# Two mixer and feed-forward layers written out, their modulation sums placed anew, and ScalarE's gates, Silus and root tables regrouped

## The chip, the cores and the metric

The kernel runs on one core of a Trainium2 chip. TensorE multiplies into PSUM banks; VectorE, ScalarE and GpSimd each work through a list of their own, in order; SyncE issues all DMAs here. The engines meet at semaphores. The metric is the device time of one execution in microseconds, lower is better.

## The reference

The program is a stack of two parts. Only the first, `first_block`, is touched by the change. All data is fp32, 256 tokens of width 1024. Cut to what matters:

```python
c_act = silu(c)
for l in range(2):                                     # DEPTH
    mod = c_act @ ada_w[l] + ada_b[l]                  # 6 x 1024: sh1 sc1 g1 sh2 sc2 g2
    h = rmsnorm(x, norm_mix_w[l]) * (1 + sc1) + sh1
    x = x + g1 * mixer(h)
    h = rmsnorm(x, norm_ffn_w[l]) * (1 + sc2) + sh2
    u = causal_dwconv(h @ w_up[l], conv_w, conv_b)     # width 2 x 2816, 3 taps
    a, val = split(u, 2)
    x = x + g2 * ((gelu(a) * val) @ w_down[l])

def mixer(h):
    # proj = h @ w_in: latents of attention, q/k/v of the mLSTM, o, its gates, g_mla, g_mlstm
    y_mla   = attention(rmsnorm(c_q) @ w_uq, rmsnorm(c_kv) @ w_ukv, rope(k_rope))
    q_m, k_m = silu(causal_dwconv([q_m, k_m]))         # 4 taps
    y_mlstm = sigmoid(o_m) * rmsnorm(mlstm(q_m, k_m, v_m, i, f))
    merged  = sigmoid(g_mla) * (y_mla @ w_br_mla) + sigmoid(g_mlstm) * (y_mlstm @ w_br_mlstm)
    return merged @ w_out
```

The second block has a modulation of its own, from two conditions (`c_2` and `c_ctx_2`); its sums are computed ahead, during the layers of the first. The block itself (recurrences, window attention, a mixture of experts) is the same before and after.

## The kernel before

**Products.** Each fp32 product is made of three: ScalarE writes the high part of a weight piece (`split_high`, line 207), VectorE the low part (`split_low`, line 212), and TensorE multiplies high by high, high by low and low by high (lines 218 to 220). So each weight piece goes through a DMA, ScalarE, VectorE and TensorE.

**Modulation.** It is no product on TensorE. A row of 1024 weights per output lies across the partitions, 128 outputs at once, and VectorE multiplies it with Silu(c) and sums up (`Modulation.add_up`, line 478), one "sum" for 128 outputs, 48 in each mixer and 24 in each feed-forward stage. The rows of weights (512 KB each) come into a ring of slots; `fetch` (SyncE) waits until the slot's last sum is done. `fetch_row` brings the broadcast condition, once for each set, and has to wait until the last sum of the set before; `bend` (line 470) is its Silu on ScalarE; the first sum of a set waits for it. The mixer's ring has three slots and its sets are 32 and 16 sums; the feed-forward's has two, its sets are 8 and 16.

**The mixer.** Its order on each engine is planned: every step of every engine is a generator that yields due times, and `in_turn` sorts them into one list for each engine. The weight pieces in order of due time: lat_a, lat_b, qk 0 to 4, uq, ukv, qk 5 to 7, v (72.4), og (85.6), br (98.8 to 148.3), branch (151.6 to 174.7), out (179.0 to 202.1), the clock ending at 205.4; a high part is due 8.0 before its product and a low part 6.8. Between the products lie eight heads of attention (63.2 + 8.2 h), eight heads of the mLSTM (86.7 + 7 h), then the division (`div_dve`, `div_act`, from t_d = 141.7), which ends with the product by the gate og, and the turn of its result (`y_turn` for b = 1, due t_d + 11). Due times give the order alone; in the run the steps come when their waits end. Before, the 48 sums are due evenly from qk 5 (61.6) to branch 0 (151.6), with an additional 2.0 ahead of the second set. `og_act` and `br_act` read PSUM with a Sigmoid on ScalarE, `conv_act` makes each Silu of the conv 4.0 behind its projection. `merge_dve` multiplies the branches by the gates. TensorE's wait for a free bank goes by `Units`.

**The feed-forward.** Its order is written by hand. The up product has 11 chunks; each has 4 tiles of 128 outputs. The down product has six chunks, numbers 11 to 16, of 8, 8, 6, 8, 8, 6 tiles of 128 hidden rows. Chunks lie in two buffers, so ScalarE and VectorE split chunk n when TensorE has done chunk n - 2, and SyncE fetches it when chunk n - 2 has been split. Behind the splits of chunks 12 to 15, VectorE makes four sums each; `read` takes the product's half and adds it to x.

**The layers.** `nc.Fori(0, DEPTH, 1)` is a loop on the chip, whose body is the mixer and the feed-forward once. The activation tables of ScalarE are loaded where a function is not in the table that is there (ACT_TABLE_LOAD in the trace).

## Time and profile before

| | us |
|---|---|
| three runs | 2169.6, 2176.22, 2178.95; median 2176.22 |
| the profiled execution | 2175.41 |
| its span, first to last instruction | 2173.6 |
| TensorE (PE) busy in the span | 1883.1 (87%) |
| VectorE (DVE) busy | 1604.6 (74%) |
| ScalarE (ACT) busy | 1115.4 (51%) |
| opening; mixer 0; feed-forward 0 | 0 to 34; 34 to 319; 320 to 546 |
| mixer 1; feed-forward 1; second block | 551 to 836; 837 to 1063; 1064 to the end |

The page cuts the span into 40 slices; of its lines these two tell of the clock granted to TensorE, in tenths, and of the busy share of the DMA engines:

```profile
PEclk9989899998998898999799986998899999999998
DMA  7577626655576744566421200003599799798897
```

All times in the rows further down are from one profiled execution, counted from its first instruction. In a timeline row stand the start, the duration, engine, line, operation, what it writes and reads, and in brackets the idle time of the engine before it and what ended that. PEclk is the granted clock of TensorE: 1.00 is the 2.4 GHz level, 0.50 the 1.2 GHz level.

### The profile page before, as it was taken

The numbers are of one execution on the slowest core, as the hardware profiler recorded it, in microseconds if no ns is written. First come the engines' busy times: TensorE is split into PE (matmuls) and PEld (weight loads), VectorE is DVE, ScalarE is ACT, GpSimd is POOL, SyncE is SP. The second block draws the span as 40 slices with busy tenths as digits, with TensorE's granted clock in tenths as the row PEclk, the third lists the DMA queues.
The fourth block names the chain that finished last, engine by engine and source line by source line (L and its number), as shares of the span: only waits on it lengthen the run. The fifth ranks groups of instructions, "written<-read, shape, count | busy, mean of one in ns | idle before, by whom it ended". The sixth has DMA issues, their size and how long they took to land. (4 is left out here: it accounts for less than half of the span.)

```text
span 2173.6 us, 32136 instructions
## 1 busy us (share of the span) xinstructions
PE 1883.1 (87%) x12662; PEld 1588.1 (73%) x12662; DVE 1604.6 (74%) x2097; ACT 1115.4 (51%) x1326; POOL 143.9 (7%) x150
## 2 busy tenths in 40 slices
PE   2888879998688878998699974998899999999998
PEld 2766668986676667996587754886788788787786
DVE  6787757976597765995548669656688688787886
ACT  2644436651564435663264342223577677676774
POOL 0000000000000000000006406500000000000000
PEclk9989899998998898999799986998899999999998
DMA  7577626655576744566421200003599799798897
GB/s 271 200 253 242 225 87 243 242 199 179 185 239 234 245 143 184 211 226 231 159 96 66 88 0 12 22 20 135 185 348 373 278 360 376 274 374 319 313 375 257
DMA packets 158134, 460.32 MB, mean 212 GB/s; under 512 B 10928, under 2 KB 13616, under 8 KB 155440
## 3 DMA queue, kind: packets, MB, share of 16 engines
q1 hardware_dynamic: 158000, 458.51, 58.9%
q8 instruction: 87, 1.43, 0.3%
q14 instruction: 47, 0.39, 0.1%
HBM read 457.42 MB, written 1.05 MB: 211 GB/s over the span
## 5 line engine op out<-in xcount | busy, mean ns | idle before, releaser
L212 DVE TENSOR_TENSOR me_wlow<-me_w,me_whigh 128x2048 fp32r<-128x2048 f32 (+1 forms) x203 | 452.0, 2247 | 107.5 <-ACT me_whigh L207 107.2
L207 ACT ACTIVATE me_whigh<-me_w 128x2048 fp32r<-128x2048 f32 (+1 forms) x203 | 380.3, 1885 | 137.8 <-PE ps L220 131.2
L218 PE MATMUL ps<-me_whigh,me_xhigh 128*128 128x512 f32 x512 | 207.5, 405 | 11.8 <-PEq L119 11.8
L218 PE MATMUL ps<-up_xhigh,ffn_whigh 128*128 128x256 f32 x704 | 202.4, 287 | 8.6 <-DVE ffn_wlow L212 7.0
L220 PE MATMUL ps<-me_whigh,me_xlow 128*128 128x512 f32 x528 | 208.7, 395 | 0.0
L219 PE MATMUL ps<-me_wlow,me_xhigh 128*128 128x512 f32 x512 | 202.5, 395 | 0.0
L219 PE MATMUL ps<-up_xlow,ffn_whigh 128*128 128x256 f32 x704 | 201.6, 286 | 0.0
L220 PE MATMUL ps<-up_xhigh,ffn_wlow 128*128 128x256 f32 x704 | 201.4, 286 | 0.0
L212 DVE TENSOR_TENSOR ffn_wlow<-ffn_w,ffn_whigh 128x2048 fp32r<-128x2048 f32 (+1 forms) x72 | 149.3, 2110 | 29.0 <-ACT ffn_whigh L207 28.7
L212 DVE TENSOR_TENSOR mix_wlow<-mix_w,mix_whigh 128x1024 fp32r<-128x1024 f32 (+2 forms) x116 | 140.1, 1211 | 29.8 <-ACT mix_whigh L207 29.8
L207 ACT ACTIVATE ffn_whigh<-ffn_w 128x2048 fp32r<-128x2048 f32 (+1 forms) x72 | 123.1, 1758 | 69.1 <-PE ps L220 69.1
L207 ACT ACTIVATE mix_whigh<-mix_w 128x1024 fp32r<-128x1024 f32 (+2 forms) x116 | 119.9, 1047 | 51.4 <-PE ps L220 32.8
L218 PEld LDWEIGHTS ps<-up_xhigh,ffn_whigh 128*128 128x128 f32 x704 | 137.6, 196 | 10.0 <-issue 9.2
L218 PE MATMUL ps<-mix_whigh,mix_xhigh 128*128 128x512 f32 (+1 forms) x320 | 137.0, 428 | 3.3 <-issue 2.0
L219 PEld LDWEIGHTS ps<-up_xlow,ffn_whigh 128*128 128x128 f32 x704 | 137.6, 196 | 0.0
L220 PEld LDWEIGHTS ps<-up_xhigh,ffn_wlow 128*128 128x128 f32 x704 | 137.6, 195 | 0.0
L219 PE MATMUL ps<-mix_wlow,mix_xhigh 128*128 128x512 f32 (+1 forms) x320 | 130.7, 409 | 0.0
L220 PE MATMUL ps<-mix_whigh,mix_xlow 128*128 128x512 f32 (+1 forms) x320 | 130.3, 407 | 0.0
L478 DVE SCALAR_TENSOR_TENSOR mix_ada_w<-mix_ada_w,mix_ada_row 128x1024 f32<-128x1024 f32 x96 | 116.7, 1218 | 11.9 <-ACT mix_ada_row L470 10.8
L218 PEld LDWEIGHTS ps<-me_whigh,me_xhigh 128*128 128x128 f32 x512 | 97.9, 191 | 33.6 <-issue 14.1
L220 PEld LDWEIGHTS ps<-me_whigh,me_xlow 128*128 128x128 f32 x528 | 100.9, 191 | 21.9
L219 PEld LDWEIGHTS ps<-me_wlow,me_xhigh 128*128 128x128 f32 x512 | 98.0, 191 | 20.4 <-issue 1.0
(658 smaller groups left out, 4204.7 us busy)
## 6 DMA issues: line engine op xcount, KB each, us to landing
me_w<-w_exp_gate SPq DMA_DIRECT2D x34, 2048.0 KB, 9.6
me_w<-w_exp_up SPq DMA_DIRECT2D x34, 2048.0 KB, 10.2
me_w<-w_exp_down SPq DMA_DIRECT2D x32, 2048.0 KB, 10.3
mix_w<-w_mix SPq DMA_DIRECT2D x108, 512.0 KB, 3.8
mix_ada_w<-ada_w SPq DMA_DIRECT2D x96, 512.0 KB, 4.9
ffn_w<-ffn_w_up SPq DMA_DIRECT2D x20, 2048.0 KB, 7.8
ffn_ada_w<-ffn_ada_w SPq DMA_DIRECT2D x48, 512.0 KB, 5.5
ffn_w<-ffn_w_down SPq DMA_DIRECT2D x8, 2048.0 KB, 7.8
```

The costliest lines, as they stand in the source:

```text
L207: return nc.scalar.activation(high, x, ACT.Copy)
L212: return nc.vector.tensor_tensor(low, x, high.bitcast(F32), ALU.subtract)
L218: nc.tensor.matmul(out, lh, rh, start=start, stop=False)
L219: nc.tensor.matmul(out, lh, rl, start=False, stop=False)
L220: return nc.tensor.matmul(out, ll, rh, start=False, stop=stop)
L478: nc.vector.scalar_tensor_tensor(out=w, in0=w, scalar=1.0, in1=self.row, op0=ALU.mult, op1=ALU.mult, accum_out=self.sums[:, i:i + 1]).then ...
```

## The change

- The layers are written out: a loop of the program that builds the kernel, not of the chip.
- Feed-forward: two slots of the ring are added in the place of `hT` (free once the input is split); behind the splits of chunks 12 to 16 VectorE makes 2, 2, 2, 2 and 8 sums; the fetches are two chunks further ahead, and the second set's row is fetched ahead of chunk 12's weights.
- Mixer: 36 sums are due from v 0 to br 13, 12 from branch 7 to 2.0 before the end; the additional 2.0 ahead of the second set is gone.
- ScalarE: the conv's Silus are made in two groups (0 to 4 and 5 to 7). og and br 0 to 2 are read with Copy; their Sigmoids are made in one group in place (`gates_bent`, due t_d + 5.0), for which the last product of the division and the merges now wait (`gated`). The turn of the mLSTM's result is due 2.5 ahead of branch 3.
- At the end of the opening, the mixer and the feed-forward's list on ScalarE, one Sqrt of a single column is made into space that nobody reads.

```diff
--- before.py
+++ after.py
@@ -442,11 +442,13 @@
 class Modulation:
 
 
-    def __init__(self, core, sem, mem, what, w, sets, slots, together=1):
-        self.w, self.sets, self.slots, self.together = w, sets, slots, together
+    def __init__(self, core, sem, mem, what, w, sets, slots, together=1, borrowed=()):
+        self.w, self.sets, self.together = w, sets, together
         self.n = sum(count for count, *_ in sets)
         self.firsts = [sum(count for count, *_ in sets[:s]) for s in range(len(sets))]
-        self.ring = core.sb(mem, f"{what}_w", [P, slots, together, DM])
+        own = core.sb(mem, f"{what}_w", [P, slots, together, DM])
+        self.ring = [own[:, i] for i in range(slots)] + list(borrowed)
+        self.slots = slots = len(self.ring)
         self.row = core.sb(mem, f"{what}_row", [P, DM])[:, :]
         self.sums = core.sb(mem, f"{what}_sums", [P, self.n])
         self.landed = [sem(f"{what}_landed{s}") for s in range(slots)]
@@ -462,7 +464,7 @@
         if j >= self.slots:
             sp.wait_ge(self.used, (j - self.slots + 1) * self.together)
         a = j * self.together
-        sp.dma_start(self.ring[:, j % self.slots], self.w[a:a + self.together].rearrange("q p f -> p q f"))\
+        sp.dma_start(self.ring[j % self.slots], self.w[a:a + self.together].rearrange("q p f -> p q f"))\
             .then_inc(self.landed[j % self.slots], 16)
 
     def bend(self, nc, act, s):
@@ -474,7 +476,7 @@
         if i in self.firsts:
             dve.wait_ge(self.row_ready, self.firsts.index(i) + 1)
         dve.wait_ge(self.landed[j % self.slots], 16 * (j // self.slots + 1))
-        w = self.ring[:, j % self.slots, q, :]
+        w = self.ring[j % self.slots][:, q, :]
         nc.vector.scalar_tensor_tensor(out=w, in0=w, scalar=1.0, in1=self.row, op0=ALU.mult, op1=ALU.mult,
                                        accum_out=self.sums[:, i:i + 1]).then_inc(self.used, 1)
 
@@ -536,6 +538,8 @@
                 act.wait_ge(reduced, 1)
                 nc.scalar.activation(sin, sin, ACT.Sin).then_inc(rotary_done, 1)
                 nc.scalar.activation(cos, cos, ACT.Sin).then_inc(rotary_done, 1)
+                act.wait_ge(ones_set, 1)
+                nc.scalar.activation(posf[:, 0:1], ones[:, 0:1], ACT.Sqrt).then_inc(rotary_done, 1)
 
             @block.vector
             def _(dve):
@@ -996,15 +1000,17 @@
         ada = Modulation(core, sem, mem, "mix_ada", layer_in("ada_w"),
                          [(CURRENT, c_rows[0:1, :], bias[:, 0:CURRENT], mod[:, NEXT:48, 0]),
                           (OTHER, c_rows[1:2, :], bias[:, CURRENT:CURRENT + OTHER], mod_next[:, 0:OTHER, 1])], 3)
-        ada_from, ada_gap = pieces.when("qk", 5), 2.0
-        ada_step = (pieces.when("branch", 0) - ada_from - ada_gap) / ada.n
+        ada_split = 36
+        ada_spans = ((pieces.when("v", 0), pieces.when("br", 13), 0, ada_split),
+                     (pieces.when("branch", 7), pieces.clock - 2.0, ada_split, ada.n))
 
         shift = mod[:, 0:KD, 0]
         norm_pe, norm_dve, norm_act, x_low = normed_features(
             core, sem, "mix_norm", x, ident, gain, shift, (rstd, diag), hT, xs, 0.0, (4, 5, 6, 4), started, readied=3)
 
         def ada_at(i):
-            return ada_from + ada_step * i + ada_gap * sum(i >= first for first in ada.firsts[1:])
+            a, b, first, end = ada_spans[i >= ada_split]
+            return a + (b - a) * (i - first) / (end - first)
 
         def ada_fetch(sp):
             for j in range(ada.n):
@@ -1480,9 +1486,11 @@
                 act.wait_ge(done, pieces.count("qk", j))
                 nc.scalar.activation(conv[:, j, :], units.bank(f"qk{j}")[:, 0:SEQ], ACT.Identity,
                                      bias=fv["conv_b"][:, j:j + 1], scale=cw[:, 24 + j:25 + j]).then_inc(tapped, 1)
-                yield last("qk", j) + 4.0
-                units.read(act, f"qk{j}")
-                nc.scalar.activation(conv[:, j, :], conv[:, j, :], ACT.Silu).then_inc(conv_silu, 1)
+                if j in (4, KD - 1):
+                    yield last("qk", j) + 4.0
+                    for i in range(0 if j == 4 else 5, j + 1):
+                        units.read(act, f"qk{i}")
+                        nc.scalar.activation(conv[:, i, :], conv[:, i, :], ACT.Silu).then_inc(conv_silu, 1)
 
         def conv_dve(dve):
             for j in range(KD):
@@ -1516,7 +1524,7 @@
             for t in range(TT):
                 yield last("og", 3) + 0.7 * t
                 act.wait_ge(done, pieces.count("og", 3))
-                units.close(nc.scalar.activation(og[:, t, :], units.bank(f"og{t}"), ACT.Sigmoid), f"og{t}")
+                units.close(nc.scalar.activation(og[:, t, :], units.bank(f"og{t}"), ACT.Copy), f"og{t}")
 
         spread, ml_masked, ml_exped, ml_scored = (sem(f"ml_{n}") for n in ("spread", "masked", "exped", "scored"))
         ml_weighed, ml_totalled, ml_read = (sem(f"ml_{n}") for n in ("weighed", "totalled", "read"))
@@ -1590,7 +1598,7 @@
 
         div_own, div_meaned, div_rooted, ml_ready = (sem(n) for n in ("div_own", "div_meaned", "div_rooted", "ml_ready"))
         t_d = ml_at(HEADS - 1, 6.0)
-        t_y[1] = t_d + 11.0
+        t_y[1] = max(t_d + 11.0, pieces.when("branch", 3) - 2.5)
 
         def div_dve(dve):
             V = nc.vector
@@ -1638,7 +1646,7 @@
             yield t_d + 8.6
             dve.wait_ge(div_own, n)
             for t in range(TT):
-                units.read(dve, f"og{t}")
+                dve.wait_ge(gated, t + 1)
                 V.tensor_tensor(sq[:, t], sq[:, t], og[:, t, :].rearrange("p (h d) -> p h d", d=HD), ALU.mult)\
                     .then_inc(ml_ready, 1)
 
@@ -1653,7 +1661,19 @@
                     yield last("br", 4 * j + 3) + 0.7 * t
                     act.wait_ge(done, pieces.count("br", 4 * j + 3))
                     units.close(nc.scalar.activation(br[:, t, j * 512:(j + 1) * 512], units.bank(f"br{j}{t}"),
-                                                     ACT.Sigmoid), f"br{j}{t}")
+                                                     ACT.Sigmoid if j == 3 else ACT.Copy), f"br{j}{t}")
+
+        gated = sem("gated")
+
+        def gates_bent(act):
+            yield t_d + 5.0
+            for t in range(TT):
+                units.read(act, f"og{t}")
+                nc.scalar.activation(og[:, t, :], og[:, t, :], ACT.Sigmoid).then_inc(gated, 1)
+            for t in range(TT):
+                for j in range(3):
+                    units.read(act, f"br{j}{t}")
+                nc.scalar.activation(br[:, t, 0:3 * 512], br[:, t, 0:3 * 512], ACT.Sigmoid).then_inc(gated, 1)
 
         merged = sem("merged")
 
@@ -1664,6 +1684,7 @@
                     for t in range(TT):
                         yield last("branch", i) + 0.8 * t
                         dve.wait_ge(done, pieces.count("branch", i))
+                        dve.wait_ge(gated, 2 * TT)
                         units.read(dve, f"br{2 * b + j}{t}")
                         bank = units.bank(f"branch{b}{j}{t}")
                         dst = m[:, t, j * 512:(j + 1) * 512]
@@ -1745,7 +1766,12 @@
                 act.wait_ge(g_spread, i + 1)
                 nc.scalar.activation(g_row[:, i * 512:(i + 1) * 512], core.ps[:, 6, :], ACT.Copy).then_inc(g_copied, 1)
 
-        residual_own = sem("residual_own")
+        residual_own, table_ahead = sem("residual_own"), sem("table_ahead")
+
+        def root_ahead_act(act):
+            yield pieces.clock
+            nc.scalar.activation(lat_rs[:, 0, 0:1], k["ones"][:, 0:1], ACT.Sqrt).then_inc(table_ahead, 1)
+
 
         def residual_dve(dve):
             for c in range(2):
@@ -1787,7 +1813,8 @@
             def _(act):
                 in_turn(norm_act(act), pieces.high_parts(nc, act), lat_read_act(act), lat_act(act),
                         gates_act(act), conv_act(act), u_read_act(act), og_act(act), head_act(act), ml_act(act),
-                        div_act(act), y_act(act, 0), y_act(act, 1), br_act(act), spread_act(act), merge_act(act),
+                        div_act(act), gates_bent(act), y_act(act, 0), y_act(act, 1), br_act(act), spread_act(act), merge_act(act),
+                        root_ahead_act(act),
                         ada_act(act))
 
 
@@ -1826,13 +1853,14 @@
         small = Carver(core.sb(mem, "ffn_small", [P, KD + TT])[:, :])
         gain, rstd, diag = small(KD), small(TT), cv[:, 4, :].rearrange("p (t n) -> p t n", n=P)
         late = slice(NEXT + OTHER, NEXT + OTHER + LATE), slice(NEXT + OTHER + LATE, 48)
-        kept = sem("ffn_kept")
+        kept, table_ahead = sem("ffn_kept"), sem("ffn_table")
         c_rows = layer_in("ffn_c")
         ada = Modulation(core, sem, mem, "ffn_ada", layer_in("ffn_ada_w"),
                          [(LATE, c_rows[0:1, :], bias[:, CURRENT + OTHER:CURRENT + OTHER + LATE], mod_next[:, late[1], 0]),
-                          (NEXT, c_rows[1:2, :], bias[:, CURRENT + OTHER + LATE:], mod_next[:, 0:NEXT, 0])], 2)
-        down_share = NEXT // 4
-        ada_ahead = {2: (0, 1), 15: range(10, 14), 16: range(14, 18), **{n: (n - 4,) for n in range(6, 14)}}
+                          (NEXT, c_rows[1:2, :], bias[:, CURRENT + OTHER + LATE:], mod_next[:, 0:NEXT, 0])], 2, 1,
+                         [hT[:, 4 * i:4 * i + 4, :].rearrange("p (q k) n -> p q (k n)", q=1) for i in range(2)])
+        down_ends = (10, 12, 14, 16, ada.n)
+        ada_ahead = {2: (0, 1), 15: (12, 13), 16: (14, 15), **{n: (n - 2,) for n in range(4, 14)}}
         tmp = flat(cv[:, 0:2, :])
         spread_diag = cv[:, 0:4, :].rearrange("p b (k n) -> p (b k) n", n=P)
         cw, cb = fv["ffn_conv_w"], fv["ffn_conv_b"]
@@ -1992,6 +2020,7 @@
             ada.bend(nc, act, 1)
             for n in range(n_up - 1 + STAGES, n_chunks):
                 split(n)
+            nc.scalar.activation(rstd[:, 0:1], k["ones"][:, 0:1], ACT.Sqrt).then_inc(table_ahead, 1)
 
         def main_dve(dve):
             yield 13.0
@@ -2054,9 +2083,8 @@
 
             for m, n in enumerate(range(n_up - 1 + STAGES, n_chunks)):
                 split(n)
-                if n < n_chunks - 1:
-                    for i in range(LATE + down_share * m, LATE + down_share * (m + 1)):
-                        ada.add_up(nc, dve, i)
+                for i in range(down_ends[m - 1] if m else LATE, down_ends[m]):
+                    ada.add_up(nc, dve, i)
                 if n == n_up + len(downs) // 2 + 1:
                     read(0)
             ada.finish(nc, dve, 1)
@@ -2071,9 +2099,11 @@
                     if n == STAGES:
                         ada.fetch_row(sp, 0)
                     for j in ada_ahead.get(n, ()):
-                        if j == LATE + 1:
-                            ada.fetch_row(sp, 1)
+                        if j == 2:
+                            sp.wait_ge(x_low, 4)
                         ada.fetch(sp, j)
+                    if n == n_up + 1:
+                        ada.fetch_row(sp, 1)
                     if n >= STAGES:
                         sp.wait_ge(low, before(n - STAGES + 1))
                     if n < n_up:
@@ -2082,7 +2112,7 @@
                         c, k0, kn = downs[n - n_up]
                         sp.dma_start(raw[:, n % STAGES, 0:kn], wd[:, k0:k0 + kn, c * half:(c + 1) * half])\
                             .then_inc(landed[n % STAGES], 16)
-                for j in range(18, ada.n):
+                for j in range(16, ada.n):
                     ada.fetch(sp, j)
 
             @block.tensor
@@ -2108,7 +2138,7 @@
         mod = core.sb(mem, "mod", [P, 48, 2])
         opening(core, I["ada_first"], I["c_first"], bias[:, 0:NEXT], I["first_b"], mod_next, **opened)
         core.settle()
-        with nc.Fori(0, DEPTH, 1) as layer:
+        for layer in range(DEPTH):
             def layer_in(name):
                 return I[name][layer]
             kk = dict(k, lat_gain=fvt[:, L_OFF["q_norm"][0]:L_OFF["kv_norm"][1]])
```

## Rows read from the trace of the kernel before

**Rows 1.** Windows: busy us (count) of PE, PEld, DVE, ACT, POOL; PEclk; DMA; GB/s
```profile
34.00:319.00 285.00, 236.08 (x1168) 191.99 (x1168) 206.55 (x382) 138.10 (x219) 0.00 (x0) 0.93 0.58 199
319.00:545.00 226.00, 205.42 (x1368) 190.77 (x1368) 169.64 (x242) 112.04 (x144) 0.00 (x0) 0.94 0.58 214
```

**Rows 2.** Waits of TensorE, 440 to 560, then 990 to 1062: total, times, longest
```profile
PE ps L218 <- DVE ffn_wlow L212: 12.7, 4, 4.2
...
PE ps L218 <- DVE ffn_wlow L212: 13.4, 4, 4.2
```

**Rows 3.** Timeline, start, us, [idle before]: VectorE and ScalarE, down product
```profile
485.71 1.23 DVE L478 SCALAR_TENSOR_TENSOR ffn_ada_w<-ffn_ada_w,ffn_ada_row 128x1024 f32<-128x1024 f32 x1 [6.95 <-DMA ffn_ada_w<-ffn_ada_w]
...
488.11 2.29 DVE L212 TENSOR_TENSOR ffn_wlow<-ffn_w,ffn_whigh 128x2048 fp32r<-128x2048 f32 x1
...
475.59 2.87 ACT L207 ACTIVATE ffn_whigh<-ffn_w 128x2048 fp32r<-128x2048 f32 x2 [1.93 <-PE ps L220]
486.47 1.91 ACT L207 ACTIVATE ffn_whigh<-ffn_w 128x2048 fp32r<-128x2048 f32 x1 [8.01 <-PE ps L220]
...
1001.98 1.91 ACT L207 ACTIVATE ffn_whigh<-ffn_w 128x2048 fp32r<-128x2048 f32 x1 [8.01 <-PE ps L220]
```

**Rows 4.** Window of the first 6.7 us after a long pause
```profile
490.00:496.70 6.70, 6.15 (x15) 4.83 (x16) 3.91 (x6) 0.18 (x1) 0.00 (x0) 0.50 0.83 269
```

**Rows 5.** Timeline, VectorE and ScalarE, around the loop's turn and its end
```profile
545.09 0.69 DVE L2053 TENSOR_TENSOR x<-x,cv 128x512 f32<-128x512 f32 x1
550.90 0.18 DVE L1085 COPY mod<-mod_next 128x16 f32<-128x16 f32 x1 [5.12 <-issue]
...
1062.67 0.69 DVE L2053 TENSOR_TENSOR x<-x,cv 128x512 f32<-128x512 f32 x1
...
1064.59 1.06 ACT L2241 ACTIVATE rw_space<-x 128x1024 f32<-128x1024 f32 x1 [27.71 <-PEq L119]
```

**Rows 6.** Timeline, ScalarE and VectorE, start of the second mixer
```profile
552.90 1.28 ACT L847 ACT_TABLE_LOAD   x1
...
552.91 0.17 DVE L867 TENSOR_SCALAR mix_small<-mix_small 128x2 f32<-128x2 f32 x1 [0.47 <-ACT mix_early L843]
```

**Rows 7.** Waits of TensorE, 34 to 320; timeline of ScalarE
```profile
PE ps L1171 <- DVE mix_latTlow L1157: 2.6, 2, 1.9
...
PE ps L218 <- DVE mix_early L1496: 1.5, 1, 1.5
...
252.81 1.08 ACT L1655 ACTIVATE mix_br<-ps 128x512 f32<-128x512 f32 x2
```

**Rows 8.** Timeline, SyncE, ScalarE, TensorE, where the second row is fetched
```profile
203.80 0.33 SPq L459 DMA_DIRECT2D mix_ada_row<-c_rows  x1
...
209.76 1.06 ACT L470 ACTIVATE mix_ada_row<-mix_ada_row 128x1024 f32<-128x1024 f32 x1 [6.88 <-DMA mix_ada_row<-c_rows]
...
211.35 0.38 PE L1289 MATMUL ps<-mix_qkT 96*128 96x128 f32 x1 [2.98 <-ACT mix_qkT L1345]
...
236.34 0.70 PE L1546 MATMUL ps<-mix_early 64*128 64x256 f32 x2 [0.71 <-DVE mix_mls L1569]
```

**Rows 9.** Timeline, VectorE and TensorE, around the division, and a window
```profile
241.24 0.29 DVE L1580 COPY mix_ml<-ps 128x130 f32<-128x130 f32 x1
...
256.80 1.12 PE L1373 MATMUL ps<-base,mix_sq 128*128 128x128 f32 x4 [4.63 <-DVE mix_sq L1642]
...
254.40:264.60 10.20, 6.40 (x18) 4.78 (x19) 7.68 (x12) 3.67 (x6) 0.00 (x0) 0.50 0.41 149
```

**Rows 10.** Window of the output product; VectorE's residual; DMA issues (KB, us to landing)
```profile
290.00:320.00 30.00, 25.02 (x120) 20.59 (x120) 18.35 (x25) 8.42 (x12) 0.00 (x0) 0.99 0.11 36
...
313.99 0.69 DVE L1759 TENSOR_TENSOR mix_sq<-ps,mix_ml 128x512 f32<-128x512 f32 x1 [5.78 <-PE ps L220]
...
ffn_w<-ffn_w_up SPq DMA_DIRECT2D x20, 2048.0 KB, 7.8
ffn_ada_w<-ffn_ada_w SPq DMA_DIRECT2D x48, 512.0 KB, 5.5
```

## The prediction

> **What bounds the kernel now.** I read the stage windows first, then what TensorE waited for in each, then the timelines around its longest waits. In the windows TensorE is busy for 236.1 of the 285 us of a mixer and for 205.4 of the 226 us of a feed-forward stage [rows 1]. VectorE (206.6 and 169.6 us) and ScalarE (138.1 and 112.0 us) have idle time in both. So TensorE sets the end, and a change is worth what it takes out of TensorE's idle time, plus what the clock loses behind each long pause: after the longest pause of rows 2 the granted clock is 0.50, the 1.2 GHz level, for 6.7 us [rows 4]. Work that ScalarE or VectorE saves elsewhere is worth nothing. The change touches only the time before about 1063 us; the second block behind it stays.
>
> **Feed-forward, the down product.** Here TensorE waits four times in each layer for the low part of the weights (VectorE line 212): 12.7 us in layer 0, 13.4 us in layer 1 [rows 2]. The timeline of VectorE shows why. Before it splits the chunk that TensorE wants it has four modulation sums to do (line 478) in a ring of two slots; the third waits 6.95 us for its DMA, ends late, and the split starts at 488.11, when TensorE has been idle since 486.4 [rows 3]. ScalarE's splits start when TensorE ends a chunk: 475.59 and 486.47, so a chunk of eight tiles takes 10.9 us at full clock [rows 3], and one of six takes 6/8 of it, 8.2 us.
> With the change only two sums (1.2 us each; the two before the split take from 485.71 to 488.11 [rows 3]) lie between two splits, and with four slots they were fetched a chunk earlier. VectorE then needs two splits of 2.2 us and two sums, 6.8 us, for a chunk, which is less than 8.2 us. By hand, from 486.4: chunk 13 ends at 494.6, 14 at 505.5, 15 at 516.4, 16 at 524.6; VectorE's splits for 14, 15 and 16 are ready at about 492.8, 501 and 511, each before TensorE needs it. The last eight sums come behind the split of chunk 16: four are there, four come at the pace of a DMA (a median of 5.5 us to landing [rows 10]), so they end at about 521, before the last read at 524.7. That is hidden by chunk 16; without that cover it would cost 3 to 5 us.
> TensorE ended at 544.3 in layer 0 and at 1061.9 in layer 1: just before the last read, a pair of operations 0.72 us apart of which rows 5 shows the second (545.09 and 1062.67). Chunk 12 ended at 486.4 and, in layer 1, at 1001.9 [rows 3]. From the end of chunk 12 that is 57.9 and 60.0 us for work of 10.9 + 10.9 + 8.2 + 8.2 = 38.2 us. Gain: 19.7 + 21.8 = **41.5 us**; 26.1 of it are the waits, the rest is clock. The bounds: all of it (42), and, if one of the four waits per layer stays at its size with its clock, 31. In front of this, the row of the second set is fetched before chunk 12's weights on SyncE's queue, so these go out some 4 us later, when VectorE has done sum 7; they are needed 16 us later. Zero.
>
> **Layers written out.** From the last addition (545.09 + 0.69) to the first operation of layer 1 (550.90) 5.1 us pass; where the loop is left it is 1.2 us (1062.67 + 0.69 to 1064.59) [rows 5]. I take the second for both: **-4 us**, bounds -3 and -4.8. The Trainium skill (Runtime: NRT & Kernel Launch, section Instruction fetch mechanics) says that a taken branch out of the fetched window costs a fetch, while straight code is streamed. The two gaps agree, and by it only the one taken branch counts, not two.
>
> **Root table ahead.** In a mixer's start the load takes 1.28 us behind the squares, and VectorE's mean is ready 0.2 us after the load begins [rows 6]: -1.0 us in layer 1, -0.8 in layer 0. In the feed-forward's start the reciprocal stands behind the copy of the gate row in VectorE's list, so I take nothing for it; bounds 0 and -1.3. Sum **-2 us**. The added Sqrt operations stand after the last work of ScalarE in their stage.
>
> **Conv Silus batched.** ScalarE no longer stops between the projections of q and k for a Silu, its table and VectorE's taps. The waits that hang on it are TensorE's 2.6 us (line 1171) and 1.5 us (line 218 on line 1496) [rows 7]. I take -2.5 us a layer. Against it: three Silus in a row now stand before a copy for head 1 (+0.8). Net -1.7 a layer, **-3.5 us**, bounds 0 and -8.
>
> **Mixers' sums moved: the second row.** Sum 32 needs another row (Silu of the other condition). Its DMA can start only when sum 31 is done, takes 5.9 us (203.80 to 209.76); ScalarE stands at its Silu for 6.88 us and VectorE at sum 32, and TensorE loses 2.98 us [rows 8]. In the plan of before a gap of 2.0 lay there (due times 118.4 for sum 31, 122.3 for 32). The change drops the gap: 132.1 and 134.0. What stands behind sum 32 on VectorE is then the split of br 13 and the mask of the last mLSTM head, which TensorE wants at about 235.6 (it waits 0.71 us there now [rows 8]). Row out at 231.2, there at 237.1, Silu 238.2, sum 32 239.4, split 240.6, sum 33 241.8, mask 242.5: a wait of some 6.7 us. So -2.98 and its 3.4 us of half clock (-1.7) go, and +6.0 and about 1.7 come: +3 in layer 0, some less in layer 1, whose old wait I take as larger: **+5 us**. Bounds: -8 (the new wait is hidden) and +14 (7 each).
>
> **The y turn and the gates.** TensorE waits 4.63 us for mix_sq and more inside the turns, with the clock at 0.50 for 10.2 us [rows 9]. The turn now comes two pieces later, and no sums lie in the division's chain. But the same edit puts five operations of ScalarE (a table, two og and two wide br Sigmoids: 1.28 + 1.1 + 2.9 = 5.3 us, by two operations of 512 columns in 1.08 us [rows 7]) behind the square root, which waits for VectorE, and ahead of the high part of branch 1, whose low part stands ahead of the rest of the division on VectorE. From the end of the last head's product, X = 241.2 [rows 9]: root X + 6.2, gates done X + 11.4, high part 12.4, low part 13.6; TensorE wants it at X + 11.1. It waits 2.5 us there, 1.5 us for branch 2, has the turns' 1.4 us, and clock. Before, "turns and branch 0 to 2 done" is at X + 26.8; after, at X + 24.1 plus some 3 of clock. **0 us**, bounds -9 and +3 a layer. TensorE's wait for the merge (mix_qk) behind branch 5 stays: the order of the merges is not changed. The Sigmoids of og and br 0 to 2 lose their loads (1.28 us each [rows 7]), but ScalarE has time there: zero.
>
> **Twelve sums in the output product.** The DMA share there is 0.11, so the rows land early enough, but 14 us are added to VectorE's 18.35 of 30 [rows 10]. They stand ahead of merges and low parts (+1 us), and with three slots and about 5 us a fetch the last is done about 1.6 us behind the point at which the residual could begin (313.99 [rows 10]), which VectorE's tail passes on: +2.5 a layer, **+5 us**, bounds 0 and +12.
>
> **Sum.** -41.5 - 4 - 2 - 3.5 + 5 + 0 + 5 = -41 us. The profiled run took 2175.4 us (a span of 2173.6 and 1.8 around it), 0.8 under the median of the runs, 2176.2. 2175.4 - 41 = 2134.4, and against the median 2135.2. Forecast: **2135 us**.
>
> **The rivals.**
> 1. *The forecast*: the down product runs through, the mixers stay within 5 us of themselves. 2125 to 2145 us. Chance 0.55.
> 2. *The mixers gain too*: the row's wait is hidden and the division's stall goes with its half clock: -8 and -18 instead of +5 and 0, so 31 us less: about 2106; half of it gives 2119. For: VectorE, busy for 206.6 of 285 us [rows 1], loses 12 sums in the part with the heads. Against: both new queues stand in the lists themselves. 0.19.
> 3. *The mixers lose*: the row's wait costs 7 us a layer and the tail 6: +16 on the forecast, 2151. 0.13.
> 4. *Weights late behind rows.* Each chunk's 2 MB takes 7.8 us to land [rows 10] and now shares the engines with rows fetched ahead; by my times chunk 15 is there only 2.6 us before it is wanted. If each of three chunks comes 4 us late in both layers, 24 us are lost with half as much clock: 2159 at the worst, 2150 in the middle. The Trainium skill (Trainium Kernel Development and Optimization, section Key Constraints) says that all queues interleave on the same 16 engines, which is what this rival needs. 0.08.
> 5. *Slower than before.* SyncE stands at a row's fetch until VectorE has used its slot, and the chunk's weights are queued behind it; VectorE stands at the split of these weights. Each of four chunks a layer would then show its whole 7.8 us: 62 us against the 41 of the sum, so 2134 + 62 = 2196, 21 above before. It decides as soon as a row's wait names a sum that comes after the split of the chunk queued behind it; by the lists, the two rows ahead of chunk 15 wait for sums 8 and 9, which come two splits before. 0.02.
> 6. *No change*: written-out code is streamed later than looped code by as much as the rest brings, 2176. Against it: the first pass of the loop, fetched afresh, took 511.8 us (34 to 545.8), the second 512.5 (550.9 to 1063.4) [rows 1, 5]. 0.03.
>
> **Numbers.** The likeliest case gives 2135. The range of 8 in 10 takes in case 1, the nearer half of 2 and most of 3 and 4: 2114 to 2152. A measurement of this kernel tells 0.5%, some 11 us, from no change: faster 0.95, same 0.03, slower 0.02.
>
> **What would show it.** Four waits of TensorE on ffn_wlow gone (under 2 us together a layer) and the clock at 1.00 from the end of the up product on; layer 1 begins about 1 us behind layer 0; ScalarE's wait for mix_ada_row still near 7 us, with a TensorE wait for the mask (line 1569) of over 5 us; no wait for mix_sq, but one for mix_wlow at branch 1 or 2. If the down product keeps waits of over 6 us a layer, or the mixers become shorter than 275 us, the prediction is wrong in that step.

## The result, and the profile after

| | before | after |
|---|---|---|
| time, median of 4 runs (range), us | 2172.9 (2166.9 to 2179.0) | **2102.7** (2100.4 to 2109.5) |
| profiled execution / its span, us | 2175.4 / 2173.6 | 2101.4 / 2099.6 |
| TensorE's mean granted clock | 0.933 | 0.947 |

The ratio is 0.967 (95% interval 0.9645 to 0.9693): 3.3% faster, some 72 us. The forecast was 2135, its range 2114 to 2152. The sign was right; the time is 11 us below the low end. The forecast's -41 us stood on a median before of 2176.2; the fourth run made it 2172.9, so some 3 us of the miss come from there.

The stages of after, in the columns of [rows 1]: one mixer with the feed-forward's norm, then the rest of that feed-forward stage.

```profile
34.00:308.00 274.00, 231.99 (x1168) 190.21 (x1168) 206.68 (x382) 131.05 (x216) 0.00 (x0) 0.94 0.62 207
308.00:513.00 205.00, 197.73 (x1368) 186.05 (x1368) 169.00 (x242) 112.29 (x145) 0.00 (x0) 0.98 0.64 236
```

Both stages are shorter. Taken between the same events of both traces: the last product of layer 0's mixer stands 270.5 us behind the opening's end at 34 (282.2 before), and layer 1's mixer is 12.5 us shorter; the feed-forward stages are 19.9 and 22.3 us shorter, the turn to layer 1 4.9, the second block 2.3. So 42.2 us come from the feed-forward stages, as forecast (41.5), and **24.2 from the mixers, where the forecast had a loss of 6.5** (-3.5 + 5 + 0 + 5), or 5.5 with the 1 us that the root's table gives layer 0.

The down product of layer 0 in after, from the end of chunk 12, as a window:

```profile
474.00:512.60 38.60, 38.59 (x171) 31.62 (x169) 30.66 (x37) 11.79 (x8) 0.00 (x0) 1.00 0.65 234
```

TensorE is busy for 38.59 of 38.60 us at a clock of 1.00. The waits of [rows 2] are gone. The prediction's sum was 38.2 us for this stretch of 57.9.

TensorE's waits in layer 0's mixer from 96 us on, after (us in total, times, longest):

```profile
PE ps L1554 <- DVE mix_mls L1577: 5.4, 3, 2.9
...
PE ps L218 <- DVE mix_qk L1693: 4.6, 1, 4.6
PE ps L218 <- DVE mix_wlow L212: 3.8, 2, 2.8
PE ps L1295 <- DVE mix_qkT L1317: 3.1, 4, 0.8
PE ps L1564 <- DVE mix_mls L1584: 3.1, 3, 1.8
PE ps L1307 <- ACT mix_att L1362: 2.0, 2, 1.7
...
PE ps L218 <- DVE mix_sq L1697: 1.4, 1, 1.4
```

And before, over the same stretch:

```profile
PE ps L1373 <- DVE mix_sq L1642: 4.6, 1, 4.6
PE ps L218 <- DVE mix_qk L1672: 4.6, 1, 4.6
PE ps L1556 <- DVE mix_mls L1576: 4.2, 3, 1.8
PE ps L1546 <- DVE mix_mls L1569: 4.2, 4, 2.9
PE ps L1289 <- DVE mix_qkT L1311: 3.4, 4, 1.1
PE ps L1289 <- ACT mix_qkT L1345: 3.0, 1, 3.0
PE ps L1295 <- ACT mix_att L1349: 2.0, 2, 1.3
PE ps L1301 <- ACT mix_att L1356: 1.9, 2, 1.6
```

Four things were forecast and are there: the long wait for mix_sq (before's line 1642) is gone, so is the one of 3.0 us behind the second row's old place (line 1345), the wait for mix_wlow at branch 1 is there (2.8 us, forecast 2.5), and the merge's 4.6 us stay. Not forecast: the waits for the exponentials of the heads (2.0 us, line 1349) are gone too, and the wait for the mask of the last head (now line 1577) is 2.9 us, 3.8 in layer 1, not 6.7. The prediction's own sign of being wrong, a mixer under 275 us, is there too: 274 us in the window above, which was 285.

To see where the mixers' time goes I took the start of the same six matmuls of the mixer in every trace, at 38.9, 96.3, 196.3, 244.9, 273.1 and 314.7 us of before's layer 0 and at the same places of layer 1. The table gives how much longer or shorter each of the five parts became against before, as a mean of both layers, in us. In one cell the two layers can differ by much (e3_gates, last heads: +3.7 and -4.3), so a mean of under 2 us tells little by itself. The experiments are those of the next section.

| kernel | to head 0 | heads | last heads, row | division, y turn | merges, output |
|---|---|---|---|---|---|
| after | -2.4 | **-8.8** | -0.7 | -2.5 | +2.7 |
| e1_silu | -2.9 | +0.1 | +1.1 | +0.4 | +0.3 |
| e2_sums | +0.8 | **-9.9** | +0.2 | -5.4 | +1.7 |
| e3_gates | +0.9 | +0.8 | -0.3 | +0.6 | -0.2 |
| e4_ffn | +0.6 | +0.8 | +1.4 | -0.2 | 0.0 |
| e5_cut | +0.5 | **-14.5** | -1.4 | -1.6 | +0.5 |
| e6_after_nogates | -1.7 | -7.8 | +1.8 | -6.2 | +1.6 |
| e7_after_merge | -3.2 | -6.8 | -0.9 | -2.3 | -4.7 |
| e8_phase | +0.6 | -9.4 | +1.1 | -6.2 | +1.7 |
| e9_early_end | +1.0 | +1.1 | -3.6 | -5.0 | +0.2 |
| e10_late_start | +0.1 | -3.9 | 0.0 | +2.5 | 0.0 |
| e11_start | +0.6 | -2.2 | -0.8 | -0.1 | 0.0 |
| e13_after_oldsums | -1.8 | -0.8 | +0.2 | +0.5 | +1.2 |
| e14_after_oldsilu | +1.0 | -7.2 | -0.9 | -2.5 | +2.6 |
| e12_split32 | -1.9 | -9.1 | -9.7 | -2.5 | -1.8 |
| e15_split32_nogates | -3.3 | -10.0 | -7.2 | -5.3 | -4.0 |

### The profile page after: what moved, and what is told of

Same layout as the page of the kernel before. It is cut to its first block and busy times, and to the rows that moved or that the text cites. A ratio compares the mean times of both kernels' runs of the same rounds, so it can differ in the third digit from the quotient of the medians.

```text
span 2099.6 us, 31490 instructions
## 1 busy us (share of the span) xinstructions
PE 1850.5 (88%) x12662; PEld 1567.1 (75%) x12662; DVE 1603.8 (76%) x2097; ACT 1102.0 (52%) x1323; POOL 143.9 (7%) x150
## 5 line engine op out<-in xcount | busy, mean ns | idle before, releaser
L207 ACT ACTIVATE mix_whigh<-mix_w 128x1024 fp32r<-128x1024 f32 (+2 forms) x116 | 119.6, 1045 | 41.5 <-PE ps L220 23.0
```

What stands on the lines that cost most here:

```text
L207: return nc.scalar.activation(high, x, ACT.Copy)
```

## The experiments

Ratios are to the kernel before, run beside each, with a 95% interval.

**Each part alone on the kernel before.** First the Silus:

```diff
-                yield last("qk", j) + 4.0
-                units.read(act, f"qk{j}")
-                nc.scalar.activation(conv[:, j, :], conv[:, j, :], ACT.Silu).then_inc(conv_silu, 1)
+                if j in (4, KD - 1):
+                    yield last("qk", j) + 4.0
+                    for i in range(0 if j == 4 else 5, j + 1):
...
```

> The kernel before with the q/k convolution's Silus batched (five, then three) and nothing else. In the changed kernel the stretch of a mixer ahead of the last mLSTM heads was about 10 us a layer shorter, where the prediction had 1.7 a layer for the Silus and nothing for the sums that left it. Theory A (the Silus do it: ScalarE no longer stands behind VectorE's taps, and TensorE's waits of 2.6, 1.5 and two of about 1 us go, with the clock behind them): about -20 us, a ratio of 0.991. Theory B (the sums that left VectorE do it, and the Silus are worth what the prediction said): -3.5 us, 0.998.

Measured: 2171.7 us, ratio 0.9987 (0.9968 to 1.0006), some -3 us and not clear of no change. Theory A falls; -3.5 us is within the interval for the edit alone. In the table its gain stands before head 0 (-3.0 and -2.9 in the two layers) and is partly given back.

Then the sums:

```diff
-        ada_from, ada_gap = pieces.when("qk", 5), 2.0
-        ada_step = (pieces.when("branch", 0) - ada_from - ada_gap) / ada.n
+        ada_split = 36
+        ada_spans = ((pieces.when("v", 0), pieces.when("br", 13), 0, ada_split),
+                     (pieces.when("branch", 7), pieces.clock - 2.0, ada_split, ada.n))
...
```

> The kernel before with the mixers' modulation sums moved (36 between v 0 and br 13, twelve in the output product, no gap ahead of the second row) and nothing else. The prediction's terms for it: +5 for the second row and +5 for the tail, so +10 us, 1.005. Theory A: the same, +5 to +10. Theory B (VectorE, freed of sums under the heads, lets TensorE run on): -16 from there, so about -8 us, 0.996, with TensorE's waits in the head stretch gone here and not in the run with the Silus alone.

Measured: 2151.7 us, ratio 0.9893 (0.9863 to 0.9922), **-23 us where the prediction had +10**. Theory B is right in its sign and too small. The heads' part as a window between the same two matmuls, columns as in [rows 1]; first before:

```profile
96.30:196.30 100.00, 84.96 (x405) 67.18 (x404) 81.52 (x160) 46.74 (x79) 0.00 (x0) 0.90 0.73 249
```

This kernel:

```profile
96.30:187.00 90.70, 79.90 (x406) 64.10 (x405) 73.64 (x146) 46.65 (x79) 0.00 (x0) 0.94 0.68 234
```

And the kernel with the sums cut, of the next experiment:

```profile
96.30:180.10 83.80, 74.96 (x405) 60.26 (x404) 51.12 (x160) 46.74 (x79) 0.00 (x0) 1.00 0.83 294
```

TensorE runs the same 405 or 406 matmuls. Its idle time falls from 15.0 to 10.8 to 8.8 us, and its busy time from 85.0 to 79.9 to 75.0, with the clock at 0.90, 0.94 and 1.00: of 16.2 us between the first and the last, 6.2 are waits and 10.0 clock. In layer 1 the same part is 12.9 us shorter.

In the first heads VectorE has next to no room. The same 172 or 173 matmuls, before and then with the sums moved:

```profile
104.00:146.00 42.00, 33.72 (x172) 27.88 (x173) 38.14 (x73) 21.49 (x36) 0.00 (x0) 0.91 0.88 298
104.00:140.00 36.00, 30.83 (x173) 26.05 (x174) 33.20 (x63) 22.36 (x37) 0.00 (x0) 0.97 0.68 233
```

VectorE is busy for 91% of the stretch before and for 92% here: five sums fewer, 4.9 us less work, and a stretch that is 6.0 us shorter. One link of the first head's chain, from the copy of q and k to the mask, before and then here:

```profile
104.27 0.68 DVE L1311 COPY mix_qkT<-ps 96x512 f32<-96x512 f32 x1
104.87 1.21 DVE L478 SCALAR_TENSOR_TENSOR mix_ada_w<-mix_ada_w,mix_ada_row 128x1024 f32<-128x1024 f32 x1
...
107.54 0.55 DVE L1318 SCALAR_TENSOR_TENSOR mix_att<-ps,consts 128x384 f32<-128x384 f32 x1
```

```profile
104.01 0.69 DVE L1313 COPY mix_qkT<-ps 96x512 f32<-96x512 f32 x1 [1.94 <-PE ps L1283]
...
106.15 0.54 DVE L1320 SCALAR_TENSOR_TENSOR mix_att<-ps,consts 128x384 f32<-128x384 f32 x1
```

It takes 3.3 us with a sum in it and 2.1 without. The division's chain on VectorE, before and then with the sums moved:

```profile
242.66 1.22 DVE L1609 TENSOR_TENSOR mix_sq<-mix_ml 128x1024 f32<-128x1024 f32 x1
243.79 1.22 DVE L478 SCALAR_TENSOR_TENSOR mix_ada_w<-mix_ada_w,mix_ada_row 128x1024 f32<-128x1024 f32 x1
244.94 0.09 DVE L478 DVE_READ_ACCUMULATOR mix_ada_w<-mix_ada_w,mix_ada_row 128x1 f32 x1
244.94 0.19 DVE L1612 TENSOR_TENSOR mix_small<-mix_small,mix_ml 128x16 f32<-128x16 f32 x1
245.03 1.22 DVE L1613 TENSOR_REDUCE mix_small<-mix_sq 128x16 f32<-128x1024 f32 x1
246.16 1.22 DVE L478 SCALAR_TENSOR_TENSOR mix_ada_w<-mix_ada_w,mix_ada_row 128x1024 f32<-128x1024 f32 x1
```

```profile
235.88 1.22 DVE L1611 TENSOR_TENSOR mix_sq<-mix_ml 128x1024 f32<-128x1024 f32 x1
237.13 0.19 DVE L1614 TENSOR_TENSOR mix_small<-mix_small,mix_ml 128x16 f32<-128x16 f32 x1
237.24 1.21 DVE L1615 TENSOR_REDUCE mix_small<-mix_sq 128x16 f32<-128x1024 f32 x1
238.49 0.18 DVE L1618 TENSOR_TENSOR mix_small<-mix_small 128x16 f32<-128x16 f32 x1
...
246.01 0.66 PE L1375 MATMUL ps<-base,mix_sq 128*128 128x128 f32 x4 [0.52 <-DVE mix_sq L1644]
```

A sum between two links delays all that follow by its 1.22 us. Without them TensorE waits 0.52 us for mix_sq, not 4.63.

The gates and the y turn (the hunks of gates_bent, the Copy in og_act and br_act, and t_y):

> The kernel before with the gates of og and br 0 to 2 taken in one batch under one table, and the y turn moved two pieces later, and nothing else. The prediction's term: 0 us (-18 to +6). The changed kernel shows the part from the last head to the end of branch 2 about 2.9 us a layer shorter: if that comes from this edit alone, -6 us, 0.997. If the sums, which still stand in the division's chain here, undo it: +3 us or more.

Measured: 2173.9 us, 0.9995 (0.9978 to 1.0012): nothing, as the prediction's term said. It is a zero of two sides: in its trace the wait of 4.6 us for mix_sq is gone, and TensorE waits 5.5 us for mix_wlow (4.8 of them at once) where it did not before.

The feed-forward's part (the hunks of Modulation's ring, down_ends, ada_ahead and the second row's fetch):

> The kernel before with the feed-forward's part alone: a ring of four for the modulation rows, sums two by two, the second row's fetch ahead of chunk 12. The prediction's term: -41.5 us (-31 to -42), a ratio of 0.981, with TensorE's waits for the low part of the weights in the down product gone. A rival by which part of that gain belongs to other edits (the mixers hand over a different clock or queue): -31 or less, 0.986.

Measured: 2130.7 us, 0.9785 (0.9752 to 0.9819), -43.5 us by the medians and -47 by the ratio, from four runs: the whole term, the rival falls. TensorE's waits in the down product are gone here as in after.

**VectorE's time or the rows' transfers?** Theories V and D differ in what a sum costs. Here each sum takes 8 of its 1024 columns (`add_up` has a new argument for that), so the kernel leaves out nearly all of the mixers' modulation and is no kernel to use.

```diff
-                    ada.add_up(nc, dve, i)
+                    ada.add_up(nc, dve, i, 8)
```

> The kernel before with each of the mixers' 48 modulation sums cut to 8 of its 1024 columns, at its old place in the list, with the same rows fetched; the modulation it gives is not the reference's. The sums moved alone took 23.5 us off, which the prediction had not seen: the heads' part of a mixer became 9.4 us shorter and the part from the last head to branch 2 6.5. Theory V (a sum of 1.22 us on VectorE stands ahead of links of the heads' and the division's chains, for which TensorE then waits at half clock behind): both gains and more come here too, -32 to -45 us, 0.982. Theory D (what counts is when the rows are transferred, beside the weights): the rows still come as before, so under -8 us, 0.997 or more.

Measured: 2142.8 us, 0.9852 (0.9827 to 0.9878), -32 us: theory V. Its heads window stands above: VectorE is busy for 51 us instead of 82, while the DMA share rises to 0.83. In the heads the transfers are not what costs.

The gain of the division did not come whole: 1.6 us a layer, where moving the sums gave 5.4. The cut sums still stand in that chain, and now VectorE reaches them before their rows have landed:

```profile
237.34 0.17 DVE L479 SCALAR_TENSOR_TENSOR mix_ada_w<-mix_ada_w,mix_ada_row 128x8 f32<-128x8 f32 x1 [1.23 <-DMA mix_ada_w<-ada_w]
```

Between 96 and 256 us it waits ten times for such a row, 12.3 us in all, and TensorE still waits 2.1 us for mix_sq. So a short sum between two links is not free either, if its data comes late.

**Which of the sums?** The same split with the 36 sums shifted, then all 48 sums kept, once ending earlier, once starting later:

```diff
-        ada_spans = ((pieces.when("v", 0), pieces.when("br", 13), 0, ada_split),
+        ada_spans = ((pieces.when("v", 0) + 0.96, pieces.when("br", 13) + 0.96, 0, ada_split),
```

> The kernel before with the mixers' sums moved as in the run of that edit alone, but the 36 sums under the heads shifted by half of their spacing (0.96 us later in the plan). The spacing of the sums under the heads is nearly that of before (1.93 for 1.83). Theory P (which sum happens to fall ahead of which link of a chain decides): the time moves by 5 us or more from that run's 2151, up or down. Theory F (the gain comes from where no sums are any more: the start of the first head, the division): it stays within 3 us of it, at 0.988 to 0.991 of before.

Measured: 2151.7 us, 0.9896 (0.987 to 0.9921): as without the shift. Theory P falls. Of theory F's two places, the start of the first head and the division, the next two runs tell.

```diff
-        ada_step = (pieces.when("branch", 0) - ada_from - ada_gap) / ada.n
+        ada_step = (pieces.when("br", 13) - ada_from - ada_gap) / ada.n
```

> The kernel before with its 48 sums closer together, so that the last comes before the division (from qk 5 to br 13 instead of to branch 0; spacing 1.63 for 1.83), start and gap as before. If the 6.5 us a layer between the last head and branch 2 come from there being no sum in the division's chain, they come here too: -13 us; the heads, with 1.4 sums more under each, should give 1 to 4 a layer back: -5 to -11 in all, about 0.996. If the whole gain of the moved sums needs fewer sums under the heads: 0 or slower.

Measured: 2158.8 us, 0.9916 (0.9894 to 0.9938), **-18 us from a single line**, more than expected. The division's part gives -5.0 a layer, as expected; the heads give only 1.1 back; and 3.6 more come where the second row is fetched. That fetch now stands earlier (191.06 us for 203.80), and the wait of 3.0 us behind it is gone from the list; that the one makes the other is argued.

```diff
-        ada_from, ada_gap = pieces.when("qk", 5), 2.0
+        ada_from, ada_gap = pieces.when("v", 0), 2.0
```

> The kernel before with its 48 sums starting at v 0 instead of qk 5 and ending at branch 0 as before, with the gap (spacing 1.62 for 1.83). If the first heads gain because no sum lies between the convolution's taps and the first scores (waits of 0.68, 1.33 us for the exponentials and the half clock behind, some 4 us by 130 us of the span), that part comes here: about -4 a layer there, and the denser sums behind give it back: 0 to -6 us, about 0.998. If 12 sums fewer are what counts, nothing comes: 1.000 or slower.

Measured: 2173.5 us, 0.9991 (0.9977 to 1.0005). At the matmul that stands at 131 us before, this kernel is 4.2 us ahead in both layers, and so is the one with the sums moved: that part of the gain belongs to the later start. It goes again where the denser sums stand: TensorE's wait for mix_sq is 5.9 us here for 4.6, and the division's part is 2.5 longer. The other 5 to 6 us a layer that the moved sums gain in the heads come behind 131 us. No run takes them apart: that they come from there being fewer sums is likely, and not shown.

**The start of the layers** (the hunks of the layer loop and of the three Sqrt operations ahead):

> The kernel before with the layers written out and the root table loaded ahead, and nothing else. The prediction's terms: -4 and -2, so -6 us, 0.997, with the gap between the layers at 6.0 us instead of 10.9 and layer 1's own length as before. Rival (written-out code is fetched later than looped code in places): 0 or slower, with TensorE gaps put down to issue.

Measured: 2166.1 us, 0.9952 (0.9936 to 0.9967), -10 us, and the forecast's -6 lies just outside the interval. The turn shrinks from 10.9 to 6.06 us of TensorE's idle time and layer 0 starts 1 us earlier, as said. The other 4 us were not forecast. In the profiled execution the largest piece of them lies in layer 0's heads, where this kernel has the operations and the waits of before:

```profile
95.40:190.30 94.90, 80.19 (x406) 63.73 (x405) 81.30 (x160) 46.76 (x79) 0.00 (x0) 0.95 0.77 262
```

Against before's window above VectorE and ScalarE are busy for the same time, TensorE idles for 14.7 us instead of 15.0, and only the clock is another, 0.95 for 0.90. Layer 1 shows +0.8 in the same part, so this piece is not in every layer. But the six runs are all below 2170 us, and the interval leaves out -6: scatter in one trace does not explain the median, and where the 4 us come from stays open.

**Undone in the changed kernel.**

> The changed kernel with the gates of og and br 0 to 2 and the y turn as before (each gate in its own Sigmoid, no batch). With the sums moved alone the part from the last head to branch 2 was 6.5 us a layer shorter, in the changed kernel 2.9. Theory G (the five operations of ScalarE ahead of the high part of branch 1 give back 3 us a layer, as the prediction's rival reading of that edit said: waits for mix_wlow of 2.8 and 1.0 us): without them -6 to -7 us against the changed kernel, about 2096, a ratio to before of 0.964. Theory N (the gates are worth nothing with the sums moved either): 2103, 0.967.

Measured: 2101.9 us, 0.9659 (0.9634 to 0.9685), the same as with them. Theory N by the time, but the table shows a side that theory G had right: the division's part is 3.7 us a layer shorter without the batch (-6.2 for -2.5). The part ahead of it is longer (+1.8 for -0.7), with a wait for the mask of 6.7 and 6.1 us in the two layers for 2.9 and 3.8. That the gates set this wait is not shown: e7_after_merge has the gates in a batch and waits 5.9 and 6.4.

> The changed kernel with the mixers' modulation sums at their old places (48 from qk 5 to branch 0, gap of 2.0 us ahead of the second row) and all else changed. If the sums' move explains the difference between prediction and measurement, this kernel comes out at 2102.7 + 23.5 = 2126, or at most at the 2135 that the prediction's sum gives with its +10 for the move taken out (2125): 2120 to 2132, ratio 0.977. If the gain comes from the parts together (the batched gates and Silus make room only with the sums moved): 2110 or less, or over 2135.

Measured: 2122.1 us, 0.9753 (0.9725 to 0.9781). Putting the sums back costs 19 us (18 by the ratios) and lands near the 2125 that the prediction's sum gives without its +10 for their move. The heads' gain goes with them (-0.8 for -8.8 a layer).

> The changed kernel with the convolution's eight Silus one by one as before. Alone on the kernel before the batch gave 2.8 us (0.9987). If it is worth the same here: 2102.7 + 3 = 2106, ratio 0.968. If it is worth more beside the moved sums, where the first heads no longer wait for VectorE but could wait for ScalarE: 2110 to 2114, 0.971.

Measured: 2112.0 us, 0.9705 (0.9678 to 0.9732). The Silus are worth 9 us here by the medians and 8 by the ratios, whose intervals overlap a little, and 3 alone. 3.4 a layer lie ahead of head 0, as alone; 1.6 lie in the heads, which is within the scatter of that part. Whether the Silus are worth more beside the moved sums is not shown.

**A better kernel.** The merges of branch 5 stood in VectorE's list ahead of those of branch 3, whose bank TensorE wants next:

```diff
-            for j in range(2):
-                for b in range(2):
+            for b in range(2):
+                for j in range(2):
```

> The changed kernel with the merges in the order of the products (both of branch output 0, then both of 1), so that the bank which the last two branch pieces open is read before the merge of branch 5. TensorE's wait of 4.61 us for mix_qk, which is the same in both kernels, should go with the half clock behind it: -4.6 to -8 us a layer, so about -12 us, 2091, a ratio to before of 0.961. If the merges, now earlier, stand ahead of low parts that TensorE wants: -4 us or less.

Measured: 2090.4 us, 0.9615 (0.9588 to 0.9641): -12, the wait is gone.

```diff
-        ada_split = 36
+        ada_split = 32
...
-                     (pieces.when("branch", 7), pieces.clock - 2.0, ada_split, ada.n))
+                     (pieces.when("branch", 4), pieces.clock - 2.0, ada_split, ada.n))
```

> The changed kernel with the merges in the order of the products, and the sums split where the row changes: the 32 of the first row between v 0 and br 13, the 16 of the second from branch 4 to the end of the output product. The second row's transfer then has the division's time, and VectorE does not stand at it ahead of the mask of the last mLSTM head, where the runs with 36 sums ahead lose 2.9 to 8.0 us of TensorE's time. Expected: that wait gone, -4 to -6 a layer against the 2090.4 of the run with the merges alone, less up to 2 a layer in the output product for four sums more: about 2083, 0.958. If the four sums more cost what the wait cost: 2090.

Measured: **2073.6 us**, 0.9523 (0.9507 to 0.9539), -17 against the kernel with the merges alone. TensorE at the last head's mask, first in after, then here:

```profile
222.21 1.22 PE L1554 MATMUL ps<-mix_early 64*128 64x256 f32 x2 [2.91 <-DVE mix_mls L1577]
```

```profile
217.38 0.70 PE L1554 MATMUL ps<-mix_early 64*128 64x256 f32 x2 [0.71 <-DVE mix_mls L1577]
```

> The kernel with the merges in the order of the products and the sums split at the row's change (2073.6, 0.9523), with the gates of og and br 0 to 2 and the y turn as before. In the changed kernel the gates gave nothing either way, because the mask's wait grew (8.0 us for 2.9) as the branch part shrank (by 3.5). With that wait gone: -3 to -4 us a layer, 2067, 0.949. If VectorE's sums of the second row now fall into the y turn: 2074 or more.

Measured: **2068.4 us**, 0.9502 (0.9476 to 0.9528), -5.2. The intervals of the two ratios overlap, but all five times lie below all five of the kernel before it. The batched gates show their price, 2.8 us a layer in the division's part. This is the best of these kernels, 34 us under after.

**The parts do not simply add.** By the medians the Silus, the sums, the gates, the feed-forward and the start gave 2.5, 22.5, 0.3, 43.5 and 10.3 us alone, 79 in all; together they gave 70. Each has an interval of several us, so no more than that is to be read from it.

## Why the prediction was wrong

**The down product, -41.5: right.** Alone -43.5; in the pair of traces -42.2. The list by hand (each chunk's low part ready before its chunk, the last sums hidden by chunk 16) is what the trace shows.

**Layers written out and the root table, -6: right in place,** -4.9 at the turn and -1 at the start. As a run of its own it measured -10 (-7 to -14), and the other 4 us are open. The prediction cited the Trainium skill (Runtime: NRT & Kernel Launch, Instruction fetch mechanics) for the taken branch; the turn agrees: from the last addition's end at 514.11 to VectorE's first operation 1.1 us pass, where it was 5.1 [rows 5]. No run tells a fetch from other costs of the loop's turn.

```profile
513.42 0.69 DVE L2082 TENSOR_TENSOR x<-x,cv 128x512 f32<-128x512 f32 x1
515.23 1.06 ACT L847 ACTIVATE mix_early<-x 128x1024 f32<-128x1024 f32 x1 [17.20 <-PEq L119]
515.26 0.18 DVE L1091 COPY mod<-mod_next 128x16 f32<-128x16 f32 x1 [1.14 <-PEq L119]
...
518.63 0.79 PE L901 MATMUL ps<-mix_diag,x 128*128 128x128 f32 x2 [6.04 <-DVE mix_diag L877]
```

**Silus batched, -3.5: right alone (-2.8), perhaps too small in company (-8 to -9).** Its bound was -8.

**Mixers' sums moved: this step failed,** by sign and by 33 us. The prediction priced the move twice, at its two new places: +5 where the second row is fetched and +5 in the output product. It gave no term to the heads, where the sums now start later and seven fewer stand in the window above, because of its first premise, that VectorE has idle time in both stages and that "Work that ScalarE or VectorE saves elsewhere is worth nothing". That was read from [rows 1], an average over a mixer (206.6 of 285 us). The heads then gave 8.8 us a layer, 17.6 in all, which the sum has at nothing.

In the heads' window VectorE is busy for 81.5 of 100 us and for 38.1 of 42 in the first heads, it works in the order of its list, and each link of a head's chain and of the division's is something for which TensorE waits a moment later. That no sum stands in the division's chain any more, the prediction did see, but it counted that in the term of the gates and set it off there against ScalarE's batch.

The two prices at the new places were nearer. The tail costs 1.5 to 1.7 us a layer (forecast 2.5): the last part is 2.7 longer in after, but 1.2 longer already with the sums at their old places, and 1.7 with the sums moved alone. The row's part is 0.7 us a layer shorter (forecast 2.5 longer, within its bounds): it landed in 4.2 us instead of the 5.9 assumed, and TensorE arrived late, at half clock (below). In the six kernels with 36 sums ahead (after, e2, e6, e7, e8 and e14) TensorE waits 2.9 to 7.2 us for that mask, so the list by hand, with 6.7 (6.9 by its own times), had the wait right and its size near the upper end. Sum 33 and the split do stand ahead of the mask, as the list had it:

```profile
212.76 0.33 SPq L461 DMA_DIRECT2D mix_ada_row<-c_rows  x1
...
217.01 1.06 ACT L472 ACTIVATE mix_ada_row<-mix_ada_row 128x1024 f32<-128x1024 f32 x1 [4.57 <-DMA mix_ada_row<-c_rows]
...
219.25 1.22 DVE L212 TENSOR_TENSOR mix_wlow<-mix_w,mix_whigh 128x1024 fp32r<-128x1024 f32 x1
220.39 1.22 DVE L480 SCALAR_TENSOR_TENSOR mix_ada_w<-mix_ada_w,mix_ada_row 128x1024 f32<-128x1024 f32 x1
...
221.87 0.28 DVE L1577 TENSOR_TENSOR mix_mls<-ps,consts 128x128 f32<-128x128 f32 x1
```

With the measured -23.3 for the +10, the prediction's own sum is 2135 - 33 = 2102, and 2102.7 was measured. That closer fit is in part luck: the Silus in company, the gates and the clock move single terms by 3 to 6 us.

**The y turn and the gates, 0: right for the edit alone (e3), and by the time for the edit in the changed kernel (e6).** But the part became 2.5 us a layer shorter, as the sums left it (-5.4) and the gates took some of that back.

**The rivals.** Rival 1, the forecast, failed by its second half, that the mixers stay within 5 us of themselves. Rival 2 (the mixers gain too, 2106 to 2119, chance 0.19) was the right one, though 2102.7 lies below it, with the reason that the prediction gave for it: VectorE loses sums in the part with the heads (12 by the prediction's count, of which seven lie in the window above). Its amounts were set on the other places (-8 for the row, -18 for the division; 1.4 and 4.9 came), and the heads' 17.6 were missing. Its chance was too low because the argument against it, "both new queues stand in the lists", speaks of what is added, and not of what is taken away. Its low end is also mis-summed: 31 us off the 2135 are 2104. Rival 3 had the wrong sign. Rivals 4 and 5 did not come: TensorE has no wait for ffn_wlow in the down product, and the Trainium skill's sentence on queues that share the engines (Trainium Kernel Development and Optimization, Key Constraints) had no price here: chunks landed in 9.5 us for 7.8 and were still in time. Rival 4's worst case leaves out the clock that it names: 24 and half as much again would be 2171, not 2159. Rival 6 did not come.

## What to carry to other kernels

A moved operation has a price at the place it goes to and at the place it leaves. If its engine works through one list, look at that stretch's busy share and timeline, not at the stage's busy share, and ask of each link of a chain that ends in the bound engine what stands directly ahead of it. Filler work belongs where no chain runs on its engine: one line that ended the sums before the division gave 18 us. And put a change of input (the second row) where nothing else waits in that engine's list; choosing the split by where the row changes, 32 and 16 instead of 36 and 12, gave another 17.

## What the runs showed of the hardware that was not expected

**The clock's level depends on more than the program's own waits in a stretch.** The changed kernel and the one with the merges reordered have the same instructions up to 245 us. From 196 to 204 us TensorE is busy without a pause in both, at a clock of 1.00, and then both have the same pause of 1.70 us (for mix_y0low). Their windows just ahead of the row's wait, in this order (the second kernel is 1.4 us behind, so the windows do not hold quite the same matmuls):

```profile
204.00:212.00 8.00, 6.30 (x23) 4.30 (x22) 5.75 (x11) 3.89 (x8) 0.00 (x0) 0.72 0.80 283
```

```profile
204.00:212.00 8.00, 6.30 (x31) 4.49 (x30) 6.63 (x14) 3.75 (x8) 0.00 (x0) 1.00 0.88 308
```

The first runs partly at 1.2 GHz (0.72), comes later to the mask and waits 2.91 us there; the second runs at 2.4 GHz (1.00), comes earlier and waits 5.87. From the matmul of line 1547 near the window's start to the one behind the mask the first takes 17.32 us and the second 17.58, though the first needed 2.7 us more for the work on the way. So a wait for something that has its own time can swallow a slow stretch ahead of it, and a wait's size alone is no measure of its price. Part of the near equality is chance: the row landed in 4.2 us in the first and in 5.5 in the second.

**The scatter is large by part and small in the whole.** In the five kernels whose sums stand as before (e1, e3, e4, e11, e13), the heads' part of one layer differs from before's by -5.1 to +3.4 us. Of e11's -5.1 nearly all is TensorE's busy time at a higher clock (0.95 for 0.90); of e3's +3.4 some 2.5 are idle time. Even the second block, the same in all kernels, took between 9.1 us less (e3) and 2.2 more (e11) than in before's trace. A reading of a few us from one part of one trace needs a second layer or a second kernel beside it.
